# A two-layer mLSTM and GLA trunk on eight cores: transposes of keys and heads move from TensorE to the DMA crossbar

## The reference, cut to what matters

```python
for i in range(DEPTH):                                  # 2 layers
    h = rmsnorm(x, norm_mix_g[i])
    x = x + (mlstm_mixer if i == 0 else gla_mixer)(h, ...)
    h = rmsnorm(x, norm_ffn_g[i])
    x = x + square(relu(h @ w1[i])) @ w2[i]             # 1024 -> 4096 -> 1024
return rmsnorm(x, final_norm_g)
# both mixers: 4 heads, q and k of 128 and v of 256 features per head, a causal
# recurrence over the tokens in chunks; with decay left out:
#   num_t  = sum_{s<=t} (q_t . k_s) v_s  +  q_t C
#   C_next = C + sum_s k_s v_s^T
# the heads are normalised, gated, laid side by side (1024 features) and multiplied by w_out
```

## Time and profile before

| | us |
|---|---|
| median of 3 runs | 1492.49 (1492.47 to 1492.66) |
| profiled execution | 1492.8 |
| its span, slowest core | 1491.4 (all cores 1488.9 to 1491.4) |
| TensorE busy | 1434.5, 96% |
| VectorE busy | 793.3, 53% |
| ScalarE busy | 582.0, 39% |
| GpSimd busy | 218.6, 15% |

### The profile page before, as it was taken

How to read it: one execution, slowest core, us unless ns; L and a number is a source line. 1 busy time by engine, 2 the same in 40 slices (tenths; PEclk the granted TensorE clock), 3 DMA queues, 4 the chain that set the end, 5 groups by cost and what they waited for, 6 DMA issues and landing times.

```text
span 1491.4 us, 23054 instructions; the slowest of 8 cores (1488.9 to 1491.4 us)
## 1 busy us (share of the span) xinstructions
PE 1434.5 (96%) x7515; PEld 692.4 (46%) x7657; DVE 793.3 (53%) x1471; ACT 582.0 (39%) x1259; POOL 218.6 (15%) x213
## 2 busy tenths in 40 slices
PE   6999999999999999999999899999999999999996
PEld 2555555444444444444444445454444444444445
DVE  2388474864434434334766866777543343343456
ACT  2596566732032031033356665675300301301344
POOL 5031021420000000002112001143200000000045
PEclk9999999999999999999999999999999999999998
DMA  9950004653044044044002200047342143100016
GB/s 159 210 142 2 1 1 57 90 77 50 12 57 54 4 60 57 1 57 57 1 1 58 58 1 1 1 57 114 57 57 32 25 57 41 17 0 1 1 57 170
DMA packets 35460, 72.97 MB, mean 49 GB/s; under 512 B 2144, under 2 KB 5392, under 8 KB 35344
## 3 DMA queue, kind: packets, MB, share of 16 engines
q0 software_dynamic: 27968, 62.03, 26.4%
q1 hardware_dynamic: 6288, 8.94, 2.2%
q10 hardware_dynamic: 1088, 0.52, 0.2%
HBM read 109.35 MB, written 8.39 MB: 79 GB/s over the span
## 4 chain that ended last, share of the span: by engine, by line
PE 87%; issue 4%; DVE 3%; ACT 3%; DMA 1%; POOL 1%; DVEq 0%; ACTq 0%; POOLq 0%
PE ps L245 86%; DMA wqk<-m_win 1%; PE ps L834 1%; DVE xn L259 1%; POOL sd L255 1%; ACT og_68 L251 1%; ACT junk L251 0%; ACT NB L251 0%; DVE oT L259 0%; DVE R_65 L259 0%; ACT hnT L251 0%; DVE xT L255 0%; ACT sq L251 0%; DVE NB L693 0%; PE ps L720 0%
## 5 line engine op out<-in xcount | busy, mean ns | idle before, releaser
L251 ACT ACTIVATE rt<-ps 128x512 f32<-128x512 f32 x256 | 152.9, 597 | 606.4 <-PE ps L245 591.8
L255 DVE TENSOR_TENSOR xT<-ps,xT 128x512 f32<-128x512 f32 (+2 forms) x336 | 222.7, 665 | 264.9 <-PE ps L245 261.3
L255 DVE TENSOR_TENSOR hid<-rt 128x512 bf16<-128x512 f32 x240 | 172.0, 718 | 225.5 <-ACT rt L251 224.9
L245 PE MATMUL ps<-xn,w1b_51 128*128 128x512 bf16 x1002 | 222.3, 379 | 1.2
L245 PE MATMUL ps<-hid,w2b_53 128*128 128x512 bf16 x1004 | 220.6, 379 | 1.1
L245 PE MATMUL ps<-xn,w1b_52 128*128 128x512 bf16 x1004 | 220.6, 379 | 1.1
L245 PE MATMUL ps<-hid,w2b_54 128*128 128x512 bf16 (+2 forms) x1008 | 195.5, 352 | 0.9
L245 PEld LDWEIGHTS ps<-hid,w2b_53 128*128 128x128 bf16 x1024 | 100.2, 98 | 120.8
L245 PEld LDWEIGHTS ps<-xn,w1b_52 128*128 128x128 bf16 x1024 | 100.2, 98 | 120.8
L245 PEld LDWEIGHTS ps<-xn,w1b_51 128*128 128x128 bf16 x1024 | 100.1, 98 | 120.3 <-issue 0.6
L245 PEld LDWEIGHTS ps<-hid,w2b_54 128*128 128x128 bf16 x1024 | 95.6, 98 | 99.3
(11 more groups left out here) (182 smaller groups left out, 1235.3 us busy)
## 6 DMA issues: line engine op xcount, KB each, us to landing
w1b_51<-w POOLq DMA_DIRECT2D x8, 1024.0 KB, 14.2
w2b_53<-w POOLq DMA_DIRECT2D x8, 1024.0 KB, 14.5
w1b_52<-w POOLq DMA_DIRECT2D x8, 1024.0 KB, 18.0
w2b_54<-w POOLq DMA_DIRECT2D x8, 1024.0 KB, 14.3
outT<-oT SPq DMA_DIRECT2D x12, 512.0 KB, 3.9
xT<-xT POOLq DMA_DIRECT2D x2, 2048.0 KB, 33.4
wst_104<-m_wout POOLq DMA_DIRECT2D x4, 1024.0 KB, 7.5
wst_107<-g_wout POOLq DMA_DIRECT2D x4, 1024.0 KB, 6.8
```

What stands on the lines that cost most here:

```text
L245: t.op("pe", lambda e: e.matmul(out, lhsT=lhsT, rhs=rhs, start=start, stop=stop), r=r, w=w, sig=sig, ns=max(cols, 64) * (1.7 if f32 else 0 ...
L251: t.op("act", lambda e: e.activation(out=out, in_=in_, func=func, **kw), r=r, w=w, ns=190 + 0.84 * n + (80 if acc is not None else 0))
L255: t.op(eng, lambda e: e.tensor_tensor(out=out, in0=in0, in1=in1, op=op), r=r, w=w, ns=170 + 1.03 * n if eng == "dve" else 200 + 2.2 * n)
```

## The change

- The eight TensorE transposes and the ScalarE copy of `S7` become one DMA transpose, 128 x 1024 bfloat16, issued on SP's queue, straight from hn into hnT. `S7` of chunk i now stands behind `P2c` of the same chunk, where before it stood in the next chunk's pass.
- The four key transposes and their copy leave `S1`; a new step `KX` issues one DMA transpose of 128 x 512 bfloat16 from kT into ktok. It stands at the head of the pass of the chunk before, or, where the next chunk begins a new group, behind the fills and ahead of S1. The last chunk needs none, as before.
- For this the layouts change: a DMA transpose writes one contiguous block, so a group's slot (xn and hnT) holds its four chunks one behind the other, each 8 x 128 values and 224 bytes of padding, and kT is laid out chunk, head, token. Users of 512 tokens (matmuls, VectorE and ScalarE writes) now address four runs of 128.
- Two buffers are no longer neighbours: the second ktok is at the end of memory with padding behind it; sm and junk move behind the first one, into the region that later holds the hidden features.
- wst is handled by block: eight loads of half the size in place of four, each free to go when its half is.
- Each transposed buffer has one semaphore that counts up, in place of one semaphore per DMA. The planner books a transpose at 1300 ns of SP and 3500 ns until it has landed. The identity matrix and its set-up go.

```diff
+    def xpose(s, out, in_, r, w, buf):
+        s.dma("sp", [(out, in_)], 0, r=r, w=w)["xp"] = buf
...
+            if u["dma"] and u["xp"]:
+                free[e] = st + 1300
+                done[n] = st + 3500
...
-    XN, XO = at("xn", [128, NG, KC, GS], BF16)
-    hnTv, _ = at("hnT", [128, NG, KC, GS], BF16, XO)
-    oT, _ = at("oT", [128, 2, KC, GS], F32, XO)
+    PAD = 224
+    CB = 2048 + PAD
+    SB = 4 * CB
+    XO = cur[0]
+    cur[0] += 4 * SB
+    xsl = [at("xn%d" % i, [128, 4, CB // 2], BF16, XO + i * SB)[0] for i in range(NG)]
+    hidX = [at("hidx%d" % i, [128, 8, GS], BF16, XO + i * SB)[0] for i in range(NG)]
+    oT = [at("oT%d" % i, [128, KC, GS], F32, XO + 2 * i * SB)[0] for i in range(2)]
...
-    kTm, _ = at("kT", [128, H, GS], BF16, M + 4096)
-    ktok = [at("ktok%d" % i, [128, H, DK], BF16, M + 8192 + 1024 * i)[0] for i in range(2)]
+    kTm, _ = at("kT", [128, 4, H, CH], BF16, M + 4096)
+    KT = [M + 8192, cur[0]]
+    cur[0] += 1024 + PAD
+    ktok = [at("ktok%d" % i, [128, H, DK], BF16, KT[i])[0] for i in range(2)]
+    junk, _ = at("junk", [128, DV], BF16, M + 9216)
...
+    def xn(s_, k):
+        return xsl[s_][:, :, k * CH:(k + 1) * CH]
+    def xc(s_, k, c):
+        return xsl[s_][:, c, k * CH:(k + 1) * CH]
+    def by_c(ap):
+        return ap.rearrange("p (c n) -> p c n", n=CH)
...
-    def wout_load(layer, rnd):
+    def wout_load(layer, k):
         v = (m_wout_d if layer == 0 else g_wout_d).rearrange("(k p) n -> p k n", p=128)
-        t.dma("pool", [(wst[layer][:], v[:, rnd * 2:rnd * 2 + 2, :])], 1048576, w=[("wst", layer)])
-        for i in range(2):
-            k = rnd * 2 + i
-            sc = ong[:, layer * 8 + k:layer * 8 + k + 1]
-            t.op("dve", lambda e, i=i, k=k, sc=sc: e.tensor_scalar(
-                out=wout[:, k, :], in0=wst[layer][:, i, :], scalar1=sc, scalar2=None, op0=ALU.mult),
-                r=[("wst", layer), ("ong",)], w=[("wout", k)], ns=750)
+        i = k % 2
+        t.dma("pool", [(wst[layer][:, i, :], v[:, k, :])], 524288, w=[("wst", layer, i)])
+        t.op("dve", lambda e: e.tensor_scalar(
+            out=wout[:, k, :], in0=wst[layer][:, i, :], scalar1=ong[:, layer * 8 + k:layer * 8 + k + 1],
+            scalar2=None, op0=ALU.mult), r=[("wst", layer, i), ("ong",)], w=[("wout", k)], ns=750)
...
-            mm(PB[a][:], wqk[:, k, c0:c0 + 128], XN[:, x, k, :], [("wqk", isk, k), ("xn", x, k)], [("B", a)],
+            mm(PB[a][:], wqk[:, k, c0:c0 + 128], xn(x, k), [("wqk", isk, k), ("xn", x, k)], [("B", a)],
...
-                mm(sc4[:, h, :], kT[:, h, cs], qT[:, h, cs], [("kT", b, h), ("qT", b, h)], [("B", SC)],
+                mm(sc4[:, h, :], kT[:, c, h, :], qT[:, h, cs], [("kT", b, h), ("qT", b, h)], [("B", SC)],
                    True, True, h == H - 1, 128)
             tt(St[p][:], sc4, tri_f[:].unsqueeze(1).broadcast_to([128, H, 128]), ALU.mult, [("B", SC), ("tri_f",)], [("St", p)], 512)
-            if i == NCH - 1:
+        def KX(s, i):
+            if i >= NCH - 1:
                 return
-            for h in range(H):
-                t.op("pe", lambda e, h=h: e.transpose(tpK[:, h, :], in_=kT[:, h, cs], identity=ident[:]),
-                     r=[("kT", b, h), ("ident",)], w=[("B", DCB)], sig=(h == H - 1), ns=64)
-            act(ktok[p][:], tpK[:, 0:4, :], AF.Copy, [("B", DCB)], [("ktok", p)], 470)
+            p, (qT, kT, b) = i % 2, s.qk_buf(i // 4)
+            t.xpose(ktok[p][:], kT[:, i % 4, :, :].rearrange("p h n -> p (h n)"), [("kT", b, h) for h in range(H)],
+                    [("ktok", p)], "ktok%d" % p)
...
-            for e8 in range(8):
-                h, e2 = e8 // 2, e8 % 2
-                t.op("pe", lambda e, h=h, e2=e2, e8=e8: e.transpose(
-                    tpS[:, e8, :], in_=hn[:, h, e2 * 128:(e2 + 1) * 128], identity=ident[:]),
-                    r=[("hn", h // 2), ("ident",)], w=[("B", SC)], sig=(e8 == 7), ns=64)
-            act(hnTv[:, x, :, c * CH:(c + 1) * CH], tpS[:, :, :], AF.Copy, [("B", SC)], [("hnT", x, c)], 1000)
+            t.xpose(xsl[x][:, c, 0:1024].rearrange("p (k n) -> p k n", n=CH), hn[:].rearrange("p h d -> p (h d)"),
+                    [("hn", 0), ("hn", 1)], [("hnT", x, c)], "hn")
...
+                late = (c == 3 and g > 0)
+                if not late:
+                    s.KX(i + 1)
                 s.S2(i)
                 s.P2a(i)
-                if i > 0:
-                    s.S7(i - 1)
                 s.S34(i, 0)
                 s.P2b(i)
                 s.S34(i, 1)
                 s.P2c(i)
+                s.S7(i)
                 s.Cst(i)
                 f()
-                late = (c == 3 and g > 0)
                 if i + 1 < NCH and not late:
                     s.S1(i + 1)
                 while fills or ex:
                     f()
+                if late:
+                    s.KX(i + 1)
                 if i + 1 < NCH and late:
                     s.S1(i + 1)
-            s.S7(NCH - 1)
```

More of the change, by code:

```diff
@@ L45, in __init__, with reg @@
         s.nd = 0
+        s.xsem = {}
         s.units, s.open = [], None
-    def reg(s, key, lo, size):
-        s.iv[key] = (lo, lo + size)
+    def reg(s, key, lo, size, n=1, step=0):
+        s.iv.setdefault(key, []).extend((lo + i * step, lo + i * step + size) for i in range(n))
     def ov(s, key):
@@ L55, in ov @@
             if key in s.iv:
-                a, b = s.iv[key]
-                r += [k for k, (c, d) in s.iv.items() if k != key and c < b and a < d]
+                r += [k for k, v in s.iv.items() if k != key and
+                      any(c < b and a < d for a, b in s.iv[key] for c, d in v)]
             s.ovc[key] = r
@@ L197, in emit @@
                 s._waits(u["eng"], u["r"], u["w"])
-                s.nd += 1
-                sem = s.es.enter_context(s.nc.semaphore("d_%d" % s.nd))
-                c = 0
+                sem, c = s.xsem.get(u["xp"], (None, 0))
+                if sem is None:
+                    s.nd += 1
+                    sem = s.es.enter_context(s.nc.semaphore("d_%d" % s.nd))
                 for o, i in u["dma"][0]:
                     c += 16
-                    e["eng"].dma_start(out=o, in_=i).then_inc(sem, 16)
+                    (e["eng"].dma_start_transpose if u["xp"] else e["eng"].dma_start)(out=o, in_=i).then_inc(sem, 16)
+                if u["xp"]:
+                    s.xsem[u["xp"]] = (sem, c)
                 s._reg((sem, c), u["r"], u["w"])
@@ L331, in slot @@
         return (g + 2 * layer) % 4
-    qx, kx, wst, hidX = [], [], [], []
+    def xn(s_, k):
[4 more added lines that the diff above has]
+        return ap.rearrange("p (c n) -> p c n", n=CH)
+    qx, kx, wst = [], [], []
     for L in range(2):
-        o3 = XO + slot(L, 3) * 8192
+        o3 = XO + slot(L, 3) * SB
         qx.append(at("qx%d" % L, [128, H, GS], BF16, o3)[0])
-        kx.append(at("kx%d" % L, [128, H, GS], BF16, o3 + 4096)[0])
-        o2 = XO + slot(L, 2) * 8192
+        kx.append(at("kx%d" % L, [128, 4, H, CH], BF16, o3 + 4096)[0])
+        o2 = XO + slot(L, 2) * SB
         wst.append(at("wst%d" % L, [128, 2, D], F32, o2)[0])
-        t.reg(("wst", L), o2, 8192)
+        for i in range(2):
+            t.reg(("wst", L, i), o2 + i * 4096, 4096)
         for h in range(H):
             t.reg(("qT", L + 1, h), o3 + h * 1024, 1024)
-            t.reg(("kT", L + 1, h), o3 + 4096 + h * 1024, 1024)
+            t.reg(("kT", L + 1, h), o3 + 4096 + h * 256, 256, 4, 1024)
     for s_ in range(4):
         for k in range(KC):
-            t.reg(("xn", s_, k), XO + s_ * 8192 + k * 1024, 1024)
-            t.reg(("hid", 4 + s_, k), XO + s_ * 8192 + k * 1024, 1024)
+            t.reg(("xn", s_, k), XO + s_ * SB + k * 256, 256, 4, CB)
+            t.reg(("hid", 4 + s_, k), XO + s_ * SB + k * 1024, 1024)
             t.reg(("hid", s_, k), M + s_ * 8192 + k * 1024, 1024)
         for c in range(4):
-            t.reg(("hnT", s_, c), XO + s_ * 8192, 8192)
+            t.reg(("hnT", s_, c), XO + s_ * SB + c * CB, CB)
     for s_ in range(2):
         for k in range(KC):
-            t.reg(("oT", s_, k), XO + s_ * 16384 + k * 2048, 2048)
+            t.reg(("oT", s_, k), XO + 2 * s_ * SB + k * 2048, 2048)
             t.reg(("w1", s_, k), W[2 * s_] + k * 2048, 2048)
@@ L364, in build @@
         t.reg(("qT", 0, h), M + h * 1024, 1024)
-        t.reg(("kT", 0, h), M + 4096 + h * 1024, 1024)
+        t.reg(("kT", 0, h), M + 4096 + h * 256, 256, 4, 1024)
     for p in range(2):
-        t.reg(("ktok", p), M + 8192 + p * 1024, 1024)
+        t.reg(("ktok", p), KT[p], 1024)
+        t.reg(("u", p), M + 9728 + p * 64, 64)
+        t.reg(("eb", p), M + 9856 + p * 64, 64)
         t.reg(("St", p), M + 14336 + p * 1024, 1024)
@@ L384, in build @@
     t.reg(("zl",), SQ, 2048)
+    t.reg(("junk",), M + 9216, 512)
+    for i in range(4, 7):
+        t.reg(("sm", i), M + 9728 + i * 64, 64)
     PB = [nc.alloc_psum_tensor("ps%d" % i, [128, 512], F32) for i in range(8)]
@@ L493, in raw_xn @@
```

(9 more changed lines are left out.)

58 lines of the change are left out of this document (26 added, 32 removed).

## The result

The changed kernel takes 1529.1 to 1532.4 us (mean 1530.2) against 1492.5 to 1492.7: 1.0252 times the time, 95% interval 1.0229 to 1.0276, or 38 us slower. The forecast was 1468, and the range ended at 1487.

The account below looks back on a forecast made before the run. TensorE was taken as the bound. Removed transposes (-21.1) and half their PSUM waits (-5.2), plus late keys (+1.2) and the single hn buffer (+0.5), gave -24.6 us from 1492.49: 1468 us, range 1460 to 1476, with rivals 1456 to 1487.

Parts of the forecast that it names:

- What bounds the kernel: Whole kernel: TensorE is the bound, busy 457.8 of 460 us in the feed-forward and about 95% in the mixers.
- the 21.1 us removed: Token mixers: 376 transposes leave TensorE's stream at 56 ns each, all counted as gain, -21.1 us.
- The PSUM waits: TensorE in the mixers: waits on transpose banks and copies total 10.4 us; half counted as gained, -5.2 us.
- Landing at about 4 us: DMA transposes on SP's queue: each lands in about 4 us, bounded by under 3.9 and 13.1 us.
- Late keys: Keys of chunks 8 and 12, both layers: 0.3 us late at each of four places, +1.2 us, bounds 0 and 38.
- The other keys: Keys of chunks 1 to 7, 9 to 11, 13, 14: hidden at 4 us landing; 5.9 us late at 13.1.
- hn as one buffer: VectorE's next P2c waits until the DMA has read hn: +0.5 us, bounds 0 and 9.7.
- Heads for the output projection: First output projection of a group reads 6.7 us after chunk 3's hn ends: landing hidden at 4 us, no cost.
- Four runs: Matmuls and VectorE on operands in four 256-byte runs: taken as 0, upper bound 25 us over 3104 matmuls.
- The slower one: Rival, mixers: transposes one after another on SP's queue pace the chunks above 15.3 us a step; 1518 us at 17; chance 0.10.
- Scaled by size: Argument against pacing: 13.1 us for 512 KB is 6.6 for 256, so key and head take 12.2 us under full load.
- The 1309 ns a square: Skill's DMA crossbar figure for a 128 x 128 transpose: twelve take 15.7 us a chunk, total about 1479 us.

Follow-up runs that it names:

- the mixed kernel with the loads held off: Changed kernel with three bulk loads per layer held behind late transposes, and transposes still beside loads back on TensorE: 1468.2 to 1469.3 us, ratio 0.9830.
- the layout kernel: Changed kernel's layout and slab-by-slab wout loads, with all 376 transposes back on TensorE and ScalarE at their earlier places: 1488.1 to 1490.5 us, ratio 0.9957.

## Why the prediction was wrong

**What bounds the kernel, and the 21.1 us removed:** right as far as the runs show it. In the mixed kernel with the loads held off, where no transpose is awaited, 17.9 us at 56 ns each were to come back, with some of the waits below, and 19 to 21 did.

**The PSUM waits, half of 10.4 us:** right in kind. In that kernel the waits on ScalarE's two copies have left the list of first waits, and a wait on R (1.9 us, 2 times) is left, of the dC matmuls themselves; what their going is worth alone was not measured.

**Landing at about 4 us, "the end with little else in flight, as in half of each mixer": the step that failed.** The value is right for that half, and better than taken: 2.5 and 3.2 us. But the transposes that something waits for lie in the other half. The earlier trace rows showed it: the DMA is idle from 112 to 224 us, while the late keys of chunk 12 come in the seventh slice (digit 4) and the end of the first mixer in the ninth (digit 5). One value for 62 transfers was the error; each site should have had the DMA digit of its own slice. The upper bound that I had, 13.1 us, was close for keys at chunk 12 (11.3 and 13.1) and too low for those of chunk 2 (19.5) and for heads (20 to 21). What makes the difference is the turns above: 66 packets of a head, each behind one of the load.

**Late keys, 1.2 us, bounds 0 to 38:** 9.8 + 5.9 us at chunk 12. Chunk 8 of both mixers, on a quiet DMA, shows no wait: there the 4 us reading held. The other keys were taken as hidden, since their issue is "an iteration ahead". Chunk 2's were not: 17.1 us, behind heads on SP and beside loads; 2.9 more at chunk 4. The 5.9 us that such keys would be late at 13.1 us stood in the prediction, but in none of its bounds.

**hn as one buffer, 0.5 us, bounds 0 to 9.7:** 9.7 + 12.0 us, at the last chunk of each mixer, of which the kernel with a buffer of its own gave 14 us back. I priced the tightest place in the rows that I had picked (chunk to chunk in the middle), not the place where the transfer is slowest; and 13.1 - 3.4 = 9.7 bounds one place, where it stood for all of them.

**Heads for the output projection, "hidden":** true of the middle groups. Chunk 15's heads, with the three loads that the last chunks release, I did not go through at all; its landing is the 9.2 us that show once hn is out of the way.

**Four runs, 0:** right: the layout with all transposes on TensorE is no slower, 40 up projections of the changed kernel that read xn in four runs start 216 ns apart as before, and VectorE's St and residual add take 685 and 689 ns as in the earlier trace rows.

```profile
349.30 8.80 PE L257 MATMUL ps<-xn_45,w1b_58 128*128 128x512 bf16 x40
357.94 0.38 PE L257 MATMUL ps<-sqb,ones_bf 128*128 128x512 bf16 x1
```

**The balance** against the layout kernel (1489 us): waits 32.8 + 2.9 + 9.7 + 12.0 = 57.4 us; slower matmuls after the five long waits, 1.7 + 2.2 + 1.4 + 1.4 + 2.9 = 9.6 us (3.62 us for eight where 1.89 is usual, 5.83 for sixteen where 3.62 is, and so on); less 21.1 us of transposes and the 5.2 us that TensorE waits there for ScalarE's copies: +40.7, against 41 by the times and 44 by the ratios.

**The rivals.** The slower one had the right sign and the wrong mechanism. Transposes do not pace the chunks: key and head together land in 5.7 us on a quiet DMA, far under 15.3. Single ones are late, six times with the 2.9 us of chunk 4. "Scaled by size" was how I argued the loaded row down; a transfer of many small packets does not scale so. The 1309 ns a square of the Trainium skill ("VectorE: DVE Perf Modes", section "The three transpose paths"), an estimated 15.7 us for the twelve, does not hold here: they are those same 5.7 us. The 261 GB/s of the Trainium skill ("DMA: Bandwidth & Descriptors", section "Latency and other measured facts") is given there for a non-contiguous middle dimension, a condition that the prediction left out; the pair is hidden on a quiet DMA as it said, but there the 384 KB take 5.7 us from issue to landing, 69 GB/s.

**The range** left out what my own bounds allowed. With both at their upper end the sum is -26.3 + 38 + 9.7 = +21 us, 1514, still short of what was measured; I cut it off at 1487, as if an unmeasured landing time could only be near its lower bound. The changed kernel missed by 62 us, and the forecast of 1468 was met by a version that takes the loads out of the transposes' way, in part by luck: some 3 to 6 us of it came with the wout slabs, which the sum had not counted.

## What to carry to other kernels

Before work is moved to the DMA, list, for each transfer that somebody waits for, what else is on the DMA at that very moment; one mean or quiet landing time misleads, since the event that releases the transfer can release a bulk load too, as at chunk 12 here. A transfer of many small packets beside bulk loads costs packets times turns, so hold the load back until it has landed, shorten the load's runs, or keep the old engine for those few sites. And look past the name of a wait: here ScalarE and VectorE were named, while a DMA still reading a single buffer held them.

## What the runs showed of the hardware that was not expected

- A DMA transpose of 128 x 512 from SBUF to SBUF lands in 2.5 us, one of 128 x 1024 in 3.2, on a quiet DMA; beside loads, at the places that are awaited, 6 to 20 and 20 to 21 us.
- The same bytes loaded in runs of a quarter of the length let a key's transpose land in 6.1 to 6.5 us in place of 11.3 to 13.1.
- A wait costs more than its length. Windows (columns as in the earlier trace rows) around the first wait of the changed kernel:

```profile
84.00:86.00 2.00, 0.00 (x0) 0.00 (x0) 1.50 (x4) 1.21 (x4) 0.67 (x1) 1.00 0.99 247
...
88.00:90.00 2.00, 0.00 (x0) 0.00 (x0) 0.00 (x0) 0.00 (x0) 1.43 (x2) 0.50 1.02 338
...
98.00:100.00 2.00, 0.00 (x0) 0.00 (x0) 0.00 (x0) 0.00 (x0) 0.00 (x0) 0.50 0.03 11
```

TensorE, idle in all three, falls from 1.00 to 0.50 (1.2 GHz) and comes back at it: its next eight matmuls take 3.62 us. In the last of these stretches the DMA is nearly idle as a mean of its 16 engines, and yet the transpose counts as landed only at 99.98. Its packets show why: from 97.6 to 98.7 us the packets stand in single file, as on one engine alone: one of the transpose (256 bytes, 18 ns) and one of the load (4096 bytes, 159 ns) in turn, until the load is through and five of the transpose follow within 0.1 us. Its last two, of 4 bytes, go at 99.04; what fills the 0.9 us from there no run shows.
